# Two transformer stacks on one Trainium2 core: ten instead of six gates by seven products, and the helpers moved around them

## What is computed

```python
def adaln(c, w, b):
    m = jax.nn.silu(c) @ w + b
    return [t[:, None, :] for t in jnp.split(m, 6, axis=-1)]

def conv_ffn(h, w_up, conv_w, conv_b, w_down):
    u = causal_dwconv(h @ w_up, conv_w, conv_b)
    gate, val = jnp.split(u, 2, axis=-1)
    return (jax.nn.silu(gate) * val) @ w_down

for i in range(DEPTH_2):
    shift1, scale1, gate1, shift2, scale2, gate2 = adaln(c, ada_w[i], ada_b[i])
    h = x * (1.0 + scale1) + shift1
    y = ...
    x = layer_norm(DN_ALPHA * x + (1.0 + gate1) * y, post_ln_g[i, 0], post_ln_b[i, 0])
    h = x * (1.0 + scale2) + shift2
    y = conv_ffn(h, ffn_w_up[i], ffn_conv_w[i], ffn_conv_b[i], ffn_w_down[i])
    x = layer_norm(DN_ALPHA * x + (1.0 + gate2) * y, post_ln_g[i, 1], post_ln_b[i, 1])
```

## Time and profile before

| | |
|---|---|
| Runs shown | 2427.74, 2428.78, 2430.93 us (median 2428.78) |
| The profiled execution's own time | 2427.72 us |
| Its span, first to last instruction | 2426.0 us |
| Mean granted clock of PE | 0.998 of full speed |
| PE busy | 2396.6 us of the span |
| DVE, ACT, POOL busy | 1601.2, 688.8, 155.7 us |
| The four stages with conditioning, pairs and down jobs | about 228 to 440, 668 to 887, 1006 to 1236, 1395 to 1629 us |

### The profile page before, as it was taken

One profiled execution on the slowest core, in us unless ns is written; L12 is line 12 of the kernel. 1 busy time (PEld: TensorE's weight loads), 2 busy tenths in 40 slices (PEclk: granted clock), 3 DMA queues, 4 the chain that ended last, 5 costly groups with the idle time before them and its releaser, 6 DMA issues.

```text
span 2426.0 us, 41510 instructions
## 1 busy us (share of the span) xinstructions
PE 2396.6 (99%) x17196; PEld 2182.9 (90%) x17196; DVE 1601.2 (66%) x3363; ACT 688.8 (28%) x1404; POOL 155.7 (6%) x268
## 2 busy tenths in 40 slices
PE   9999999999999999999999999999999999999998
PEld 7879999987889898999998999898889999889998
DVE  6653877566289837698744499954456985427983
ACT  3451110144211121532032232123423331443321
POOL 2000100000031000001000041012000000000000
PEclk9999999999999999999999999999999999999999
DMA  7935995574389646598454399643334545434552
GB/s 219 238 95 180 336 311 177 154 188 111 115 308 332 234 149 187 195 318 299 148 178 131 114 329 319 233 148 122 105 122 140 174 158 167 129 105 165 166 166 96
DMA packets 403270, 458.36 MB, mean 189 GB/s; under 512 B 50751, under 2 KB 374776, under 8 KB 403084
## 3 DMA queue, kind: packets, MB, share of 16 engines
q1 hardware_dynamic: 370098, 340.53, 44.7%
q0 software_dynamic: 29936, 112.73, 12.9%
q10 hardware_dynamic: 3050, 2.46, 0.4%
HBM read 451.48 MB, written 1.29 MB: 187 GB/s over the span
## 4 chain that ended last, share of the span: by engine, by line
PE 88%; DVE 8%; DMA 1%; issue 1%; ACT 1%; POOL 0%; DVEq 0%; SPq 0%; ACTq 0%; POOLq 0%
PE job_bank L990 35%; PE job_bank L1066 26%; PE job_bank L1045 11%; PE mix_bank L1045 4%; PE job_bank L1535 4%; DVE sb_arena L2894 2%; DVE sb_arena L2938 1%; PE mix_bank L1482 1%; PE job_bank L1510 1%; PE mix_bank L1454 1%; DVE sb_arena L3003 1%; PE mix_bank L1496 1%; PE mix_bank L1021 0%; PE mix_bank L1826 0%; PE job_bank L1258 0%
## 5 line engine op out<-in xcount | busy, mean ns | idle before, releaser
L990 PE MATMUL job_bank<-sb_h,sb_ring 128*128 128x256 f32 x3616 | 807.6, 380 | 0.7 <-DVE sb_h L3173 0.7
L990 PEld LDWEIGHTS job_bank<-sb_h,sb_ring 128*128 128x128 f32 x3616 | 674.3, 189 | 100.1 <-issue 10.0
L2894 DVE SCALAR_TENSOR_TENSOR sb_arena<-sb_arena,sb_c_act 128x512 f32<-128x512 f32 x336 | 252.6, 752 | 10.6
L3003 DVE SCALAR_TENSOR_TENSOR sb_arena<-sb_arena,sb_par 128x256 f32<-128x256 f32 x440 | 195.0, 484 | 9.2 <-ACT sb_arena L2061 5.2
L1045 PE MATMUL job_bank<-sb_h,sb_ring 128*128 128x128 f32 x1600 | 184.1, 275 | 1.4 <-ACT sb_h L2360 1.4
L1045 PEld LDWEIGHTS job_bank<-sb_h,sb_ring 128*128 128x128 f32 x1600 | 181.2, 192 | 1.8 <-issue 1.6
L2061 ACT ACTIVATE sb_arena<-sb_arena,sb_par 128x256 f32<-128x256 f32 x220 | 120.2, 593 | 155.5 <-DVE sb_arena L2970 145.2
L1066 PE MATMUL job_bank<-sb_h,sb_ring 128*128 128x128 f32 x1152 | 152.7, 276 | 1.6 <-ACT sb_kept L2022 1.6
L1066 PE MATMUL job_bank<-sb_t,sb_ring 128*128 128x128 f32 x1152 | 152.8, 276 | 0.0
L1066 PEld LDWEIGHTS job_bank<-sb_h,sb_ring 128*128 128x128 f32 x1152 | 144.4, 192 | 7.3 <-issue 2.5
L1066 PE MATMUL job_bank<-sb_arena,sb_ring 128*128 128x128 f32 x1184 | 150.5, 277 | 0.0
(11 more groups left out here) (508 smaller groups left out, 3171.5 us busy)
## 6 DMA issues: line engine op xcount, KB each, us to landing
sb_arena<-in_ada_w POOLq DMA_DIRECT2D x96, 1024.0 KB, 7.3
sb_ring<-in_ffn_w_up SPq DMA_DIRECT2D x88, 1024.0 KB, 5.4
sb_ring<-in_w_up SPq DMA_DIRECT2D x44, 1024.0 KB, 5.9
sb_ring<-in_ffn_w_down SPq DMA_DIRECT2D x32, 1024.0 KB, 5.2
sb_ring<-in_w_in SPq DMA_DIRECT2D x24, 1024.0 KB, 6.1
sb_ring<-in_w_down SPq DMA_DIRECT2D x16, 1024.0 KB, 5.4
sb_ring<-in_hg_w_in SPq DMA_DIRECT2D x16, 1024.0 KB, 5.5
sb_ring<-in_ml_w_up SPq DMA_DIRECT2D x16, 1024.0 KB, 5.4
```

The lines of the kernel that those rows point to most:

```text
L990: mm = pe.matmul(o, st, mv, start=(k0 + k == 0 and t == 0), stop=(k0 + k == kn - 1), skip_group_check=True)
L2894: ins = vec.scalar_tensor_tensor(out=o, in0=w, scalar=col, in1=o, op0=ALU.mult, op1=ALU.add)
L3003: ins = vec.scalar_tensor_tensor(out=o, in0=fraw[:, i % 2, v, j:j + T], scalar=pcol(column, (l * FFN_TAPS + j) * width + c), in1=o, op0=AL ...
```

## The change

Gates 1 to 10 are fast in the first two layers of the second stack. `rescale_x` of that feed-forward is taken from DVE and done by ACT, one tile per pair, in all four layers of the second stack. PE's first two pairs of `ada_quad` stand behind jobs 9 and 17 of `fast_ups` (values 4 and 8), where they stood behind 11 and 19, and the last two behind d2's first products. DVE's two late `ada_half` stand behind d1's third weight forms and the addition of d0, still ahead of d2's first weight forms. POOL makes one operation of `tap_weights` or `gate_weights` after each transfer from the ninth on, where all stood in one block. The semaphore `form_third` is merged into `form_first`. Row forms for d1's third unit go to `t2`.

```diff
-FAST_PAIRS = (2, 3, 5, 6, 8, 9)
+FAST_PAIRS = tuple(range(1, 11))
...
-        cond_fform = [token_forms(fcv_at, 8), token_forms(fraw_at, 8), token_forms(ada_at + 8 * quarter_n, 6)]
+        cond_fform = [token_forms(fcv_at, 8), token_forms(fraw_at, 8),
+                      t2[:, 0:6, :].rearrange("p k t -> p (k t)").rearrange("p (f k c) -> p f k c", f=4, c=P)]
...
+                beside = tap_weights() if layer == L1 - 1 else gate_weights() if layer == L2 - 1 else iter(())
                 for c in range(ADA_UNITS):
-                    if layer == L1 - 1 and c == 8:
-                        tap_weights()
-                    if layer == L2 - 1 and c == 8:
-                        gate_weights()
+                    if c >= 8:
+                        next(beside, None)
...
                 def condition(n):
-                    if n in (11, 19):
+                    if n in (9, 17):
                         ada_quad()
                         ada_quad()
...
                     last_products(d1, u, *over_f(u))
+                first_products(d2, 1, *over_f(1))
+                first_products(d2, 2, *over_f(2))
                 ada_quad()
                 ada_quad()
-                first_products(d2, 1, *over_f(1))
-                first_products(d2, 2, *over_f(2))
...
+            def scale_x(l, k):
+
+                n = 2 * l
+                act.activation(x[:, k, :], x[:, k, :], ACT.Identity, scale=lnp[:, n % 2, 2, k:k + 1],
+                               bias=lnp[:, n % 2, 3, k:k + 1]).then_inc(s.x_scaled, 1)
...
                     if stack == 2:
                         raw_out(stack, l, i, 2, u)
                         first_tap(stack, l, i, 2)
+                        if 0 < i <= KD:
+                            scale_x(l, i - 1)
...
                 if stack == 2:
-                    rescale_x(2 * l)
+                    due(s.h_ready, 2 * KD)
...
                 row_forms(fact[:, 8:16, :], cond_fform[1])
                 more_forms(1)
-                if stack == 2:
-                    norm_columns(2 * l + 1)
-                ada_half()
-                ada_half()
                 row_forms(fact[:, 16:FT, :], cond_fform[2])
+                more_forms(1)
                 if stack == 1:
                     add_to_x(downs[0], 0)
                 else:
+                    norm_columns(2 * l + 1)
+                    vec.wait_ge(s.x_scaled, due(s.x_scaled, KD))
                     gated_to_x(downs[0], 0, l, 1)
                     gather(downs[0], 0)
-                more_forms(1)
+                ada_half()
+                ada_half()
                 for i, job in ((1, downs[1]), (2, downs[2])):
                     more_forms((3, 0)[i - 1])
```

More of the change, by code:

```diff
@@ L247, in __init__ @@
         self.form_first = sem("form_first")
-        self.form_third = sem("form_third")
         self.form_last = sem("form_last")
@@ L255, in __init__ @@
         self.tap_ready = sem("tap_ready")
+        self.x_scaled = sem("x_scaled")
 def weight_plan(a):
@@ L879, in gate_weights @@
                                             ALU.mult))
+                    yield
                 for c, terms in ((0, [(2, o) for o in range(BLK)]),
@@ L1079, in first_products @@
                 quarter(bank[:, 3, :], a11, rows[:, 0:kt // 2, 0:P], u == 0)
-                pe.wait_ge(s.form_first, f + 1)
+                pe.wait_ge(s.form_first, 2 * f + 1)
                 pe.wait_ge(s.tform_ready, n_t + 1)
                 quarter(bank[:, 1, :], form_slot(unit)[0][:, 0:kt // 2, :], forms[:, 0, :, :])
-                pe.wait_ge(s.form_third, f + 1)
+                pe.wait_ge(s.form_first, 2 * f + 2)
                 pe.wait_ge(s.tform_ready, n_t + 2)
@@ L2081, in fast_glu @@
                     first_tap(2, l, i, 0, gates[i])
+                    if i <= KD:
+                        scale_x(l, i - 1)
                     held = values[i]
@@ L2938, in weight_forms @@
                 vec.tensor_tensor(f[0], a21, a22, ALU.add).then_inc(s.form_first, 1)
-                own(s.form_first, form_no[unit] + 1)
-                vec.tensor_tensor(a21, a11, a21, ALU.subtract).then_inc(s.form_third, 1)
+                own(s.form_first, 2 * form_no[unit] + 1)
+                vec.tensor_tensor(a21, a11, a21, ALU.subtract).then_inc(s.form_first, 1)
                 step(vec.tensor_tensor(f[1], f[0], a11, ALU.subtract))
@@ L3119, in fast_glu @@
                 more_forms(1)
-                rescale_x(n)
+                due(s.h_ready, 2 * KD)
                 for i, (g, u) in enumerate(zip(gates, values)):
```

## The result

The changed kernel takes 2436.72 us (median of 7 runs, 2434.57 to 2437.88) against 2428.78 us (median of 7 runs beside it, 2426.98 to 2431.38): ratio 1.0029, 95% interval 1.0018 to 1.0041 (the two medians alone give 1.0033). It is 0.3% slower. The forecast was 2429.5 us; the measured median lies 0.2 us above its range and is nearest to the rival of POOL's operations, 2436.1 us. The profiled execution took 2435.43 us, its span is 2433.6 us, 7.6 more than before.

A forecast was written before the change was run, and what follows sets the result against it. PE bounds the kernel, busy 2396.6 of 2426.0 us; with ten fast gates DVE is slower. -5.9 + (1.4 + 1.6) + (2.1 + 1.6) = +0.8 us: 2428.5 profiled, 2429.6 median, stated as 2429.5; range 2423.5 to 2436.5 us.

The forecast's parts named there:

- the rival of POOL's operations: Fourth stage: each of POOL's fifteen operations holds DVE up for its whole length, 6.5 us more, 2436.1 us; chance 0.18.
- the likeliest case: Third and fourth stage: the change as drawn, DVE-bound, about even with the kernel before; chance 0.50.
- What PE is spared: Pairs of the third and fourth stage: a gate by seven products spares PE 0.65 us, eight of them 5.2 us.
- The second stage, -5.9 us: Spreading POOL's five tap operations gives back the third pair's loss, 19.08 to 13.16 us, clock included; 5.9 us gained.
- The third stage, +1.4 and +1.6: DVE makes d2's first form later, ending that piece 1.4 us later; a clock fall behind PE's wait costs 1.6 us.
- the ledger of DVE: Stage start to d2's first form: 14.9 us added, 2.7 taken away, against own waits of 10.7 (third), 8.4 us (fourth).
- The fourth stage, +2.1 and +1.6: DVE makes d2's first form later, ending that piece 2.1 us later; a clock fall behind PE's wait costs 1.6 us.
- Spread, the same operations meet the same kind of DVE work: I take 4.0 us again, nothing added: Fourth stage: POOL's fifteen operations, spread, cost DVE the same 4.0 us as in one block.
- Its own sign, a wait of 7 us and more: What would show POOL's rival: PE waiting 7 us and more ahead of d2's first quarter, in the fourth stage alone.
- What I read of the idle time: Three rows of PE's waits, for forms and `keep_mid`, make almost half of its 29.4 us of idle time.
- Edits at nothing: Last two layers, merged semaphore, row forms in `t2`, wait for `x_scaled` and late sums cost nothing.

The follow-up runs named there:

- e7_before_tap_spread: The kernel before with only POOL's five tap-weight operations spread over the second stage's pairs: 2426.38 us.
- e5_six_gates: The changed kernel with the old list of six gates by seven products, all other edits kept: 2421.70 us.
- e1_gates_block: The changed kernel with the gates' weights on POOL in one block again, tap weights still spread: 2432.69 us.
- e2_no_gate_weights: The changed kernel without POOL's operations that make the gates' weights, a constant written in their place: 2428.63 us.
- e8_late_sums: The changed kernel with the conditioning sums behind jobs 12 and 20 again, as before the change: 2438.16 us.
- e10_dve_rescale: The changed kernel with the rescaling of x on DVE again in the third and fourth stage: 2442.66 us.

## Why the prediction was wrong where it was

*The direction and the likeliest case.* I gave 0.57 to no measurable difference and 0.23 to slower; it is slower by 0.3%. The sum was +0.8 us for the profiled execution, measured +7.7. By the marks the second stage gave 0.9 us less than forecast, the third lost 0.7 more, the fourth 5.0 more.

*What PE is spared.* Right: gates at 0.65 us; the third stage's pairs took 134.84 us, forecast about 134.5.

*The second stage, -5.9 us.* Its third pair came back to 13.16 us as forecast (707.99 to 721.15), but the stage gave 5.0. I had counted an operation as holding DVE for at most its 1.9 us; it cost a form 2.4, and small waits of 0.45 and 1.06 us were left. The missing 0.9 us is no more than one execution's marks can be off. e7_before_tap_spread gained 3.0 us by the spread alone, with an interval that reaches 5.1; whether another edit adds to this stage stays open.

*The third stage, +1.4 and +1.6.* Right: +3.7 measured, with a wait of 5.43 us where 5.3 was forecast, a form without any wait of DVE ahead of it, and a lower clock behind, which cost 1.4 us. e5_six_gates confirms the ledger of DVE.

*The fourth stage, +2.1 and +1.6.* This is the step that failed, at "Spread, the same operations meet the same kind of DVE work: I take 4.0 us again, nothing added". The spread cost DVE 6.7 us of busy time in place of 4.0 in the pairs, and d2's form came 175.0 us behind the start of pair 1 in place of the 171.5 forecast (167.7 before). With the block, in e1_gates_block, it came as forecast: PE used it at 171.65. The new `keep_mid` waits (4.3 of the 4.5 us are in this stage) add nothing of their own, since they lie ahead of PE's wait for the form and shorten it. The clock does add: it stayed low until 1591 us. From the wait's end to the end of that piece PE took 1598.78 - 1584.14 = 14.64 us, and 11.6 would have done at the full clock: 3.0 us where I had priced a fall at 1.6. So +8.7 is 3.7 forecast, 3.5 for the form, 1.4 for the clock, and 0.1 unassigned. e1_gates_block and e2_no_gate_weights show the cause: 4.0 us for spreading, some 1 us of it the clock's, and 8.1 for having the operations there.

*The rival of POOL.* It named the place and half of its reason; that its +7.3 came so near was in part luck. It set 6.5 us more on the fourth stage, which lost 5.0 more, and the rest came from the other two stages. Its own sign, a wait of 7 us and more, did not come: the wait was 6.14 us, because the `keep_mid` waits stood ahead of it. DVE did not lose all of POOL's time (6.7 of 9.45 us); the three multiplications beside taps cost it their whole length or more, the ten sums less. By the Trainium skill ("SBUF — State Buffer", section "Who interferes with whom") the two exclude each other for a whole instruction; the taps' 1.1 to 1.4 us for 1.09 agree with it. The block's 4.0 us for 10.5, and taps of 1.87 us beside a sum of 0.72, do not agree with it as a price for every operation. I did not weigh that a spread places each operation behind its transfer, and so always behind a half, where it meets the taps.

*What I read of the idle time.* The three rows of waits are 10.9 of 29.4 us, a good third and not almost half; nothing in the sum rests on it.

*Edits at nothing.* The last two layers: right, 790.54 against 790.51 us. The sums' place: right, by e8_late_sums. The rescaling: it was inside the ledger at 2.7 us a stage, and e10_dve_rescale measured 5.9 for both. The halves' place cost nothing new, but the prediction passed over what stood right beside it: d2's first form behind 7.3 us of work that nobody was waiting for.

## What to carry to other kernels

When the helper engine is slower per step than the engine that it feeds, look at what stands in its queue ahead of the next thing that is waited for: moving one set of forms ahead of deferrable work gained 18.0 us with ten gates and 6.9 with six, either more than the 5.2 us of work that eight gates by the faster algorithm spare PE. Price work on GpSimd beside VectorE by which instructions it will meet, not by its average over a block, and if possible put it where VectorE has slack. Try such an algorithm after the order has been mended: with the old order ten gates cost 12 to 15 us against six; with the new one and POOL out of the way they came out some 2 us ahead, which is not proven.

## What the runs showed of the hardware

Waits of the same length end in different spans at the lower clock. In slices of 1 us the granted clock is below 1.00 from 1184 to 1188 in the changed kernel behind its wait of 5.43 us, but from 1182 to 1190 in e2_no_gate_weights behind one of 5.42. Timeline of PE in e2_no_gate_weights:

```profile
1184.78 2.07 PE L1058 MATMUL job_bank<-sb_arena 128*128 128x128 f32 x8 [5.42 <-DVE sb_arena L2940]
1186.64 3.35 PE L1058 MATMUL job_bank<-sb_arena,sb_ring 128*128 128x128 f32 x16
1189.83 1.95 PE L1058 MATMUL job_bank<-sb_arena 128*128 128x128 f32 x16
```

The same three quarter products that took 4.1 us took 5.05 here, so that this fall cost 2.4 us in place of 1.4; the one in the changed kernel's fourth stage cost 3.0, the one in e1_gates_block's 1.8. In e5_six_gates waits of 1.86 and 1.87 us, for the first form behind the halves, brought none; in the fourth stage of the kernel before and of e7_before_tap_spread one of 1.85 and one of 1.87 did. The five kernels with forms first have no wait of PE over 2.0 us in the four stages, and their clock does not fall before the last 6 us of the span. The Trainium skill ("TensorE: Matmul & The Clock Gate", section "What's actually happening") says that the gate's observation runs free of the kernel; equal waits with unequal ends agree with it.
